# Seven products of quarters for the gate and up projections of both feed-forwards

## What is computed

```
def swiglu(hn, w_ffn_in, w_ffn_out):
    a, b = jnp.split(hn @ w_ffn_in, 2, axis=-1)
    return (jax.nn.silu(a) * b) @ w_ffn_out

D_FF = -(-8 * D_MODEL // (3 * 256)) * 256        # 2816
# of each block, last step:
    ff = swiglu(rmsnorm(h, norm_ffn_pre[l]), w_ffn_in[l], w_ffn_out[l])
    h = h + rmsnorm(ff, norm_ffn_post[l])
```

## Time and profile before

| | us |
|---|---|
| runs | 1861.24, 1861.27, 1862.39 |
| median | 1861.27 |
| span of the profiled execution | 1859.4 |
| repeated part of the first feed-forward, groups 2 to 11 with their down units | about 305 |
| the same of the second feed-forward | about 305 |

### The profile page before, as it was taken

One profiled execution on the slowest core, in us unless ns is written; L12 is line 12 of the kernel. 1 busy time (PEld: TensorE's weight loads), 2 busy tenths in 40 slices (PEclk: granted clock), 3 DMA queues, 4 the chain that ended last, 5 costly groups with the idle time before them and its releaser, 6 DMA issues.

```text
span 1859.4 us, 25253 instructions
## 1 busy us (share of the span) xinstructions
PE 1830.0 (98%) x10074; PEld 1586.4 (85%) x10074; DVE 1132.7 (61%) x1553; ACT 739.9 (40%) x927; POOL 33.5 (2%) x33
## 2 busy tenths in 40 slices
PE   9999999999999999999999999999999999999996
PEld 8898989889898888988888888888898888888885
DVE  7567566753736537357565454557898775554547
ACT  5666676532322333233442222224545742222222
POOL 2000000000000000000000000000000000000000
PEclk9999999999999999999999999999999999999998
DMA  4111111132122222222422222232476413222221
GB/s 184 38 64 59 45 45 46 59 112 103 46 90 79 90 96 72 70 69 91 161 69 95 105 93 90 90 113 88 114 183 170 126 69 113 90 93 104 96 91 46
DMA packets 25973, 170.07 MB, mean 91 GB/s; under 512 B 2736, under 2 KB 5040, under 8 KB 6320
## 3 DMA queue, kind: packets, MB, share of 16 engines
q1 hardware_dynamic: 24176, 156.51, 24.5%
q0 software_dynamic: 1728, 12.58, 3.3%
HBM read 154.40 MB, written 2.10 MB: 84 GB/s over the span
## 4 chain that ended last, share of the span: by engine, by line
PE 90%; DVE 5%; ACT 2%; issue 2%; DMA 0%; POOL 0%; DVEq 0%; SPq 0%; ACTq 0%
PE psum L600 28%; PE psum L601 28%; PE psum L602 28%; DVE normed L1738 1%; PE psum L751 1%; PE psum L802 1%; PE psum L797 1%; DVE h L1828 1%; ACT w_hi L1159 1%; ACT X_hi L1159 0%; PE psum L823 0%; DMA h<-in_xfm 0%; PE psum L1080 0%; ACT std L1159 0%; ACT sq L1159 0%
## 5 line engine op out<-in xcount | busy, mean ns | idle before, releaser
L600 PE MATMUL psum<-X_hi,w_hi 128*128 128x512 f32 (+2 forms) x1648 | 590.7, 358 | 3.1 <-issue 1.5
L602 PE MATMUL psum<-X_hi,w_lo 128*128 128x512 f32 (+2 forms) x1648 | 584.0, 354 | 0.0
L601 PE MATMUL psum<-X_lo,w_hi 128*128 128x512 f32 (+2 forms) x1648 | 584.0, 354 | 0.0
L1159 ACT ACTIVATE w_hi<-w_raw 128x2048 fp32r<-128x2048 f32 x133 | 253.8, 1909 | 357.9 <-PE psum L602 357.9
L600 PEld LDWEIGHTS psum<-X_hi,w_hi 128*128 128x128 f32 x1648 | 309.6, 188 | 51.5 <-issue 6.8
L1721 DVE TENSOR_TENSOR w_lo<-w_raw,w_hi 128x2048 fp32r<-128x2048 f32 x121 | 277.0, 2290 | 119.8 <-ACT w_hi L1159 119.8
L601 PEld LDWEIGHTS psum<-X_lo,w_hi 128*128 128x128 f32 x1648 | 310.0, 188 | 45.1 <-issue 2.4
L602 PEld LDWEIGHTS psum<-X_hi,w_lo 128*128 128x128 f32 x1648 | 309.6, 188 | 43.3
L1982 DVE TENSOR_TENSOR acc<-acc,psum 128x512 f32<-128x512 f32 x176 | 115.2, 685 | 46.9 <-PE psum L602 46.8
L600 PE MATMUL psum<-M_hi,w_hi 128*128 128x512 f32 (+2 forms) x376 | 141.4, 376 | 0.0
L601 PE MATMUL psum<-M_lo,w_hi 128*128 128x512 f32 (+2 forms) x376 | 141.0, 375 | 0.0
(11 more groups left out here) (308 smaller groups left out, 2795.3 us busy)
## 6 DMA issues: line engine op xcount, KB each, us to landing
w_raw<-in_units SPq DMA_DIRECT2D x140, 1024.0 KB, 4.8
w_lo<-w_raw POOLq DMA_DIRECT2D x12, 1024.0 KB, 7.3
h<-in_xfm SPq DMA_DIRECT2D x4, 528.0 KB, 5.2
h<-in_xfm SPq DMA_DIRECT2D x1, 2112.0 KB, 9.1
decay<-in_dec SPq DMA_DIRECT2D x4, 512.0 KB, 4.7
out<-h SPq DMA_DIRECT2D x4, 264.0 KB, 2.2
out<-h SPq DMA_DIRECT2D x2, 496.0 KB, 2.9
rot<-in_consts SPq DMA_DIRECT2D x1, 528.0 KB, 13.0
```

The lines of the kernel that those rows point to most:

```text
L600: nc.tensor.matmul(dst, w2[0], x2[0], start=first, stop=False, skip_group_check=True)
L601: nc.tensor.matmul(dst, w2[0], x2[1], start=False, stop=False, skip_group_check=True)
L602: m = nc.tensor.matmul(dst, w2[1], x2[0], start=False, stop=last, skip_group_check=True)
L1159: return nc.scalar.activation(out_, in_, f, **kw)
```

## The change

In groups 4 to 11 of both feed-forwards (`FIRST7 = 3`), the gate and the up unit are computed another way. The product of weights (1024 x 256) and tokens (1024 x 512) is seen as one of 2 x 2 quarters: weights of 512 x 128, tokens of 512 x 256. The eight products of quarters are replaced by seven, of which some take sums of quarters on either side (the Winograd form of Strassen's scheme). `Q_unit` lays the weights out by quarters.

- Tokens: four sums of quarters of the normed tokens are made once for each feed-forward, in groups 2 and 3 (`token_sums` on DVE, five steps of four operations of 128 x 256), split in high and low (`T_hi`, `T_lo`, in operations of 1024 columns; one of them overwrites a quarter of `X_hi` and `X_lo`).
- Weights: four sums for each unit. POOL makes `s3` and `s1` (`first_sums`, the second in place in `w_raw`), DVE `s2` and `s4` (`sums_of`), each 128 x 512; ACT makes the high part of three of them (`sums_hi`, 128 x 1536), DVE the low (`sums_lo`). The one made in place is split with the unit itself.
- Products: `seven` issues 7 x 4 tiles x 3 matmuls of 256 columns. After four products PE waits for `u2` of DVE, goes on accumulating in the same banks, then for `u3` and `c22`.
- Results: the four quarters of a unit are combined on DVE (`chain`, `corner22`, `corner21`, `corner12`) with two copies by ACT (`takes`). `chain` is two DVE operations of 128 x 256, `u2` (the first product, copied by ACT, plus the second) and `u3` (`u2` plus the third), each waiting for the one before; the three corners are one such operation each. `deviate` multiplies the gate by `std`, `gated` by the sigmoid (128 x 512 each), and one product of 1024 columns makes the hidden values.
- PSUM: seven banks in turn in these groups, three strips for each of the two units.
- `rot`, a table of the first mixer, moves in memory, and its load is issued two unit loads later; `h_sq` shares `gate_in`; `M_hi` and `M_lo` are aligned to 512 bytes, not 2048.

The core of the diff:

```diff
-STRIPS = {"P": 2, "R": 4, "D": 8}
+STRIPS = {"P": 2, "R": 4, "D": 8, "S": 3}
+
+
+FIRST7 = 3
+PAIRS7 = FF_PAIRS - FIRST7
+HT = SEQ // 2
 
...
+        ("ffn1", "PPDPPD"),
+        ("ffn", "SSDSSD" * 3),
+        ("ffn9", "SSDSSD"),
...
+        turn += sum(2 if k == "S" else STRIPS[k] for k in kinds)
...
+        if self.depth == 7:
+            return (j + 2) % 7
+        return (self.turn + j) % self.depth * max(1, 4 // self.depth)
 
...
-    h_sq = sb("h_sq", [P, SEQ], F32, ffns)
+    h_sq = gate_in[:, 0, :]
...
+    T_hi = sb("T_hi", [P, 3, DT // 2, HT], F32R, ffns, 256)
+    T_lo = sb("T_lo", [P, 3, DT // 2, HT], F32R, ffns, 256)
...
+    wx_hi = [sb(f"wx_hi{n}", [P, 3, UNIT // 4], F32R, ffns) for n in range(2)]
+    wx_lo = [sb(f"wx_lo{n}", [P, 3, UNIT // 4], F32R, ffns) for n in range(2)]
+    up_in = sb("up_in", [P, 2, SEQ], F32, ffns)
...
+            def first_sums(at, j, idx):
+
+                slot = at.ring(j)
+                q = quarters(w_raw[slot])
+                pool.wait_ge(w_loaded[slot], 16 * (at.loads(j) + 1))
+                if not (type(idx) is int and idx == 0):
+                    pool.wait_ge(wx_lo_ready, idx)
+                nc.gpsimd.tensor_tensor(wx_raw[:, 1, :], q[:, 0, :], q[:, 2, :], ALU.add).then_inc(*wx_first.step("s3"))
+                pool.wait_ge(wx_first.sem, wx_first.at("s3", idx))
+                nc.gpsimd.tensor_tensor(q[:, 2, :], q[:, 2, :], q[:, 3, :], ALU.add).then_inc(*wx_first.step("s1"))
+            tag = "_2" if n else ""
...
+            def seven(at, j, s, idx):
+                def taken(n):
+                    pe.wait_ge(strip_free, at.strip(s + n) - 4)
+                weights_ready(at, j)
+                slot = at.ring(j)
+                own = [quarters(w) for w in (w_hi[slot], w_lo[slot])]
+                added_to = [wx_hi[slot], wx_lo[slot]]
+                early, late = slice(META, META + HT), slice(META + HT, FULL)
+                r1, r3 = (psum[:, at.bank(s), HT * i:HT * (i + 1)] for i in range(2))
+                r4, r2 = (psum[:, at.bank(s + i), 0:HT] for i in (1, 2))
+                def product(dst, ws, q, x, first, last, sig):
+                    for k in range(DT // 2):
+                        mm3(dst, [w[:, q, k * P:(k + 1) * P] for w in ws], x(k), first and k == 0,
+                            last and k == DT // 2 - 1, sig if k == DT // 2 - 1 else None)
+                def own_x(lower, cols):
+                    return lambda k: split(X_hi, X_lo, ALL, lower + k, cols)
+                def sum_x(t):
+                    return lambda k: split(T_hi, T_lo, ALL, t, k, ALL)
+                half = DT // 2
+                taken(0)
+                product(r1, own, 0, own_x(0, early), True, False, None)
+                product(r3, added_to, 0, sum_x(1), False, True, c7_pe.step("P6"))
+                taken(1)
+                product(r4, added_to, 1, own_x(0, late), True, False, c7_pe.step("P7"))
+                taken(2)
+                product(r2, own, 2, sum_x(0), True, False, c7_pe.step("P5"))
+                pe.wait_ge(c7_dve.sem, c7_dve.at("u2", idx))
+                product(r1, own, 1, own_x(half, early), False, True, (strip_done, 1))
+                pe.wait_ge(c7_dve.sem, c7_dve.at("u3", idx))
+                product(r4, own, 3, sum_x(2), False, True, (strip_done, 1))
+                pe.wait_ge(c7_dve.sem, c7_dve.at("c22", idx))
+                product(r2, added_to, 2, own_x(half, late), False, True, (strip_done, 1))
+            def two(at, k0):
+                whole = type(k0) is int and k0 == 1
                 for m in range(2):
-                    up(at, 3 * m, 12 * m)
-                    down(at, 3 * m + 2, 12 * m + 4, i0 + m, m)
+                    if whole:
+                        up(at, 3 * m, 12 * m)
+                    else:
+                        for c in range(2):
+                            seven(at, 3 * m + c, 14 * m + 3 * c, index7(n, k0 + m, c))
+                    down(at, 3 * m + 2, 12 * m + 4 if whole else 14 * m + 6, base + k0 - 1 + m, m)
...
+            pe.wait_ge(t_sums.sem, t_sums.at("t3_lo", n))
+            loop(pe, 3, lambda i: two(Place("ffn" + tag, i, 6, 28, 7), FIRST7 + 2 * i))
+            two(Place("ffn9" + tag, depth=7), FF_PAIRS - 2)
...
+            def sums_hi(at, j, idx):
+                act.wait_ge(wx_second.sem, wx_second.at("s4", idx))
+                a(wx_hi[at.ring(j)][:, :, :], wx_raw[:, :, :], ACT.Copy).then_inc(wx_hi_ready, 1)
...
+            def takes(at, s, idx, dst):
+                r1 = psum[:, at.bank(s), 0:HT]
+                act.wait_ge(c7_pe.sem, c7_pe.at("P6", idx))
+                a(dst[:, 0, 0:HT], r1, ACT.Copy).then_inc(*c7_act.step("a"))
+                strips(at, s)
+                act.wait_ge(c7_dve.sem, c7_dve.at("u2", idx))
+                a(dst[:, 0, 0:HT], r1, ACT.Copy).then_inc(strip_free, 1)
+            def two(at, k0, final):
                 for m in range(2):
+                    k, s = k0 + m, 14 * m
+                    last = final and m == 1
+                    takes(at, s, index7(n, k, 0), gate_in)
+                    strips(at, s + 2)
+                    split_hi(at, 3 * m)
+                    for c in (1, 0):
+                        act.wait_ge(g_dve.sem, g_dve.at(f"g{c}", PAIRS7 * n + k - FIRST7))
+                        a(silu_a[:, c, :], gate_in[:, c, :], ACT.Sigmoid).then_inc(*f_act.step(f"sig{1 - c}"))
+                    takes(at, s + 3, index7(n, k, 1), up_in)
+                    strips(at, s + 5)
+                    if not last:
+                        sums_hi(at, 3 * m + 1, index7(n, k + 1, 0))
+                    split_hi(at, 3 * m + 1)
+                    act.wait_ge(f_dve.sem, f_dve.at("prod", base + k))
+                    hidden(base + k, (m + 1) % 2)
+                    if not last:
+                        sums_hi(at, 3 * m + 2, index7(n, k + 1, 1))
+                    strips(at, s + 13)
...
+            def sums_of(at, j, idx):
+                q = quarters(w_raw[at.ring(j)])
+                dve.wait_ge(wx_first.sem, wx_first.at("s1", idx))
+                v.tensor_tensor(wx_raw[:, 0, :], q[:, 0, :], q[:, 2, :], ALU.add).then_inc(*wx_second.step("s2"))
+                dve.wait_ge(wx_second.sem, wx_second.at("s2", idx))
+                v.tensor_tensor(wx_raw[:, 2, :], q[:, 1, :], wx_raw[:, 0, :], ALU.add).then_inc(*wx_second.step("s4"))
+            def sums_lo(at, j, idx):
+                dve.wait_ge(wx_hi_ready, idx + 1)
+                v.tensor_tensor(wx_lo[at.ring(j)][:, :, :], wx_raw[:, :, :], as_f32(wx_hi[at.ring(j)][:, :, :]), ALU.subtract)\
+                    .then_inc(wx_lo_ready, 1)
...
+            def two_whole(at):
+                i = base + 1
+                gate_up(at, 0, 0, i)
+                for which in ("b12", "t1", "t2"):
+                    token_sums(which)
+                add_down(at, 4, range(3))
+                split_lo(at, 1)
+                hidden_lo(i, 1)
+                add_down(at, 4, range(3, 6))
+                token_sums("t4")
+                add_down(at, 4, range(6, DT))
+                token_sums("t3")
+                split_lo(at, 2)
+                gate_up(at, 3, 12, i + 1, between=lambda: [token_lo(t, name, scale) for t, (name, scale) in
+                                                           enumerate((("t1", 1.0), ("t2", -1.0), ("t4", -1.0)))])
+                sums_of(at, 4, index7(n, FIRST7, 0))
+                dve.wait_ge(t_high.sem, t_high.at("t3_hi", n))
+                v.tensor_tensor(late_half(X_lo), T3_raw, as_f32(late_half(X_hi)), ALU.subtract).then_inc(*t_sums.step("t3_lo"))
+                sums_lo(at, 4, index7(n, FIRST7, 0))
+                add_down(at, 16, range(3))
+                split_lo(at, 4)
+                sums_of(at, 5, index7(n, FIRST7, 1))
+                add_down(at, 16, range(3, 6))
+                hidden_lo(i + 1, 0)
+                sums_lo(at, 5, index7(n, FIRST7, 1))
+                add_down(at, 16, range(6, DT))
+                split_lo(at, 5)
...
+                    chain(at, s, g, gate_in)
+                    corner22(at, s, g, gate_in)
+                    corner21(at, s, gate_in)
+                    deviate(1)
+                    corner12(at, s, gate_in)
+                    deviate(0)
+                    split_lo(at, 3 * m)
+                    chain(at, s + 3, u, up_in)
+                    gated(1)
+                    gated(0)
+                    corner22(at, s + 3, u, up_in)
+                    if not last:
+                        sums_of(at, 3 * m + 1, index7(n, k + 1, 0))
+                    corner21(at, s + 3, up_in)
+                    corner12(at, s + 3, up_in)
+                    dve.wait_ge(strip_free, at.strip(s + 5) + 1)
+                    dve.wait_ge(c7_dve.sem, c7_dve.at("c22", u))
+                    dve.wait_ge(f_dve.sem, f_dve.at("act1", i))
+                    v.tensor_tensor(silu_a[:, :, :], silu_a[:, :, :], up_in[:, :, :], ALU.mult)\
```

(64 more changed lines are left out.)

151 lines of the change are left out of this document (112 added, 39 removed).

## The result

| | median us | lowest to highest | runs |
|---|---|---|---|
| before | 1861.53 | 1860.82 to 1863.30 | 20 |
| changed | 1864.22 | 1863.33 to 1865.23 | 20 |

The ratio of the changed kernel to the one before is 1.0014, with a 95% interval of 1.0007 to 1.0020: 2.7 us more, inside the 0.2% that counted as no change, and 10.3 us above the forecast of 1853.9.

A forecast was written before the change was run, and what follows sets the result against it. PE, busy 98% of the span, was the bound. Each feed-forward: 1.4 - 7 x 0.83 = -4.4 us, both -8.8; plus 1.4 for waits, 1859.4 becomes 1852.0, with 1.9 around it 1853.9; range 1847 to 1874.

The forecast's parts named there:

- The products: PE's matmuls in a unit: 84 of 256 columns at 0.1198 us replace 48 at 0.2267, gaining 1.63 us a group.
- DVE's work and the tight stretch: From up unit's end to next gate's `u2`: DVE ends at 17.29 us, PE waits 0.8 a group, period 31.8.
- For the forecast that is free: POOL's weight-sum adds, taken as 1.2 us each, end before `s2` wants them and so cost nothing.
- Port: Rival, chance 0.28: POOL's adds and DVE operations with both inputs in SBUF exclude each other; 0.7 us a group, time 1868.
- Its 0.4 for the gate's adds: Gate's adds meet `deviate` and the down unit's low part; what else shifts makes 0.4 us a group under the rival.
- its 2.4 for the entry: At the entry, four POOL adds of 1.2 us hold DVE up for half their time, 2.4 us, under the rival.
- The entry: Group 3 into 4: PE waits 1.0 us for a strip and 1.9 for `u2`; group 4 takes 34.0, 1.4 more.
- the 1.4 that I had added for extra waits: DVE operations with three waits in front, priced by no row: 0.1 us a group, 1.4 in all.
- Token sums, weight loads, `rot`: Token sums fall where DVE is half idle, counted as zero; weight loads land ahead of their splits, `rot`'s load costs nothing.

The follow-up runs named there:

- the last two runs: On the kernel with `u2` first: four strips at the entry, tokens' low parts between the products with `std`, 1840.80 us; plus low part behind `corner22`, 1839.08 us.

## Why the prediction was wrong

**The products: right.** 0.12 us each, and a group without waits is 31.06 us, where 32.64 - 1.63 = 31.0 was forecast.

**DVE's work and the tight stretch: right to 0.05 us.** With POOL's adds taken away the excess is 0.80 us where the text had 0.8, and the period 31.85 where it had 31.8. No wait of the up unit was forecast, and there was none. `u2` ends 17.30 us after the up unit there (1104.92 to 1121.81 and 0.41 more); the text had 17.29. The dependent pair `s2`, `s4` takes 1.34 us, the text had 1.32.

**"For the forecast that is free": the step that failed.** The adds take 1.32 us, near the 1.2 I took, and each is in time by its own length. But that sentence looks only at when the sum is wanted, not at what DVE does meanwhile. The adds and DVE's operations on two SBUF tiles exclude each other, and that takes 0.5 us a group in the first feed-forward, 0.3 in the second, and 2.7 and 2.8 us at the entries, where the run without the sums shows 1.4 and 1.6 of it and rows the rest. The forecast named this as the rival *Port* and gave it 0.28. In the tight stretch the rival was right in mechanism and size: the first add ends as DVE comes to the low part, which is held for 0.15 us, the second waits for the low part (held for 1.9 us; the text had 2.2), and `s2` for that, 0.08: 0.23 us where the text had some 0.3. Its 0.4 for the gate's adds, a guess, was 0.28 in the first feed-forward and 0.1 in the second; its 2.4 for the entry was near the 2.7 and 2.8. So it gave 1868 where 1864.2 came. I had set its chance low because no row of before had POOL reading beside DVE. That is no evidence against it. The Trainium skill states the rule (SBUF — State Buffer, § Who interferes with whom), and the trace now agrees with both halves: operations with both inputs in SBUF were held until POOL's add had ended, those with one input in PSUM kept 1.27 us for two. That the one which starts first holds up the other for its whole length stands on the same page (§ SBUF: two separate sides), and the rows of `w_lo` and of the second add agree: 1.16 us of add after the 2.43 us row.

**The entry: 34.0 forecast, 36.7 measured; the same step.** DVE left the up unit of group 3 late. Its rows and POOL's there, and then DVE's of the run with the low part one step later, where POOL makes no sums:

```profile
997.95 2.83 DVE L1889 TENSOR_TENSOR w_lo<-w_raw,w_hi 128x2048 fp32r<-128x2048 f32 x1 [2.50 <-ACT w_hi L1276]
1000.70 2.38 DVE L2453 TENSOR_TENSOR silu_a<-silu_a,gate_in 128x512 f32<-128x512 f32 x2
1003.00 3.48 DVE L1906 SCALAR_TENSOR_TENSOR T_lo<-t_raw,T_hi 128x1024 fp32r<-128x1024 f32 x3
1006.41 1.27 DVE L2460 TENSOR_TENSOR silu_a<-silu_a,psum 128x512 f32<-128x512 f32 x2
...
998.71 3.22 POOL L653 TENSOR_TENSOR w_raw<-w_raw 128x512 f32<-128x512 f32 x1
```

```profile
998.44 2.29 DVE L1874 TENSOR_TENSOR w_lo<-w_raw,w_hi 128x2048 fp32r<-128x2048 f32 x1 [2.50 <-ACT w_hi L1261]
1000.65 1.29 DVE L2438 TENSOR_TENSOR silu_a<-silu_a,gate_in 128x512 f32<-128x512 f32 x2
1001.85 3.49 DVE L1891 SCALAR_TENSOR_TENSOR T_lo<-t_raw,T_hi 128x1024 fp32r<-128x1024 f32 x3
1005.26 0.68 DVE L2445 TENSOR_TENSOR silu_a<-silu_a,psum 128x512 f32<-128x512 f32 x1
```

The up unit ended at 1005.43 in the first and at 1005.93 in the second. POOL's adds for the first unit hold the low part (2.83 for 2.29 us) and the products with the sigmoid (2.38 for 1.29). So the tokens' low parts, for which the text counts nothing, end after the up unit, both products follow from 0.98 on, and the weight sums start at 2.35 (2.20 in the second feed-forward). Without POOL's adds the low parts end ahead of the up unit, and the first weight sum starts at 0.99, where the text had 1.2: nothing was the right price for them, as long as nothing holds what stands ahead of them. Moving them forward, in the last two runs, cures the same delay with the hold still there: their weight sums start at 0.99 too. The run without GpSimd's sums kept these two adds (sums from 2.39 and 2.24 on), and so its bank wait was still 2.2 and 2.1 us where I had 1.0; its `u2` wait was 1.9, as forecast. Its entries of 35.3 and 35.2, less the 1.4 and 1.2 by which the sums start late, make 33.9: the forecast's 34.0. No run takes away these two adds alone, so this share is worked out from rows. They agree in a second place: 2.2, less the 1.4, plus four more adds of 0.72 on DVE, is 3.7, and the bank wait with all sums on VectorE was 3.7.

With the other adds the bank wait became 3.2 us, and the clock fell after it, a term that the sum did not have at all. Here it cost little, because DVE sets the moment of `u2` whatever PE does before: in the first feed-forward PE lost 1.5 us to the lower clock, and its wait for `u2` shrank from 1.9 to 0.4.

**The account.** Against the forecast span of 1852.0: the later groups 3.8 and 2.4, the entries 2.7 and 2.8, less the 1.4 that I had added for extra waits and that did not come, make 10.3; measured are 10.0 (span 1862.0). POOL's adds are 8.2 of it by the spans of 1862.0 and 1853.8, and 2.6 more by the delay ahead of the entries; DVE's own work in the later groups is 0.5; less the 1.4 that is 9.9.

**Token sums, weight loads, `rot`: right, or nothing to be seen.** The period ahead of the entry, in which the token sums fall, is 32.64 us as before, and no PE wait names a weight load.

## What to carry to other kernels

Before work goes to GpSimd, write down what VectorE runs in the same microseconds: an add there of 1.3 us that "fits" can hold a 2.2 us operation and be held by it, and the price appears where VectorE is short of time. Where VectorE's order decides, find the operation that PE waits for and ask which long one ahead of it is wanted later; moving one low part behind three short steps was worth more (up to 43 us, with the falls of the clock that went) than any shift of load between engines. When two waits in a row hang on the same engine, count the work ahead of the second before the first is taken away. And when a run takes work out to price it, list what it leaves in: here two adds of each feed-forward stayed, at the one place where they made the entry late.

## What the runs showed of the hardware

- Exclusion. Wherever the rows of a GpSimd add of 128x512 in SBUF and of a VectorE operation with both inputs in SBUF overlap by more than 0.1 us, one of them is longer than alone: 2.29 us became up to 3.4, 0.69 up to 1.8, and 1.3 up to 3.25. The 62 `acc<-acc,psum` beside an add in the changed kernel took 0.68 us, as the 106 others did. The time held is inside the row of the instruction, so no idle time points at it; the mean of a group against its shortest row does. In the changed kernel's groups (line, op, shape, busy us and mean ns, idle):

```profile
L1889 DVE TENSOR_TENSOR w_lo<-w_raw,w_hi 128x2048 fp32r<-128x2048 f32 x121 | 294.9, 2438 | 59.6 <-ACT w_hi L1276 59.3
...
L651 POOL TENSOR_TENSOR wx_raw<-w_raw 128x512 f32<-128x512 f32 x32 | 42.4, 1326 | 467.6 <-DMA w_raw<-in_units 296.4
L653 POOL TENSOR_TENSOR w_raw<-w_raw 128x512 f32<-128x512 f32 x32 | 77.0, 2405 | 2.5
```

- The clock. PE's granted clock fell to the lower level for 3.4 or 6.8 us after single waits of PE in an otherwise full stretch. Of the 68 waits from 0.6 to 1.9 us in the feed-forwards of the changed kernel and the experiments none was followed by it; of the 32 between 2.0 and 2.4 us, 14 were; of the 14 of 3.0 us and more, all but one. What decides between two equal waits of 2.14 us these runs do not show. A fall for 3.4 us cost PE 1.4 to 1.5 us on top of the wait; how much of it reached the time hung on the wait behind it, as at the entries.
- A matmul of 256 columns with its own weights is 0.120 us against 0.227 for 512, with the tokens as the moving side too.
